# A prefetch hint for the closing jump of TensorE's loop over three experts

## The chip, the cores and the metric

The kernel runs on one core of one Trainium2 chip. The metric is the device time of one execution in microseconds (us). Engines are called as the profile calls them: TensorE (PE; PEld for its weight loads, PEldq for its sequencer's own instructions), VectorE (DVE), ScalarE (ACT), GpSimd (POOL) and SyncE (SP), which issues the large transfers.

## What is computed

A stream of 512 tokens by 1024 features goes through two layers. Layer 0 is a gated mixer over positions and then a mixture of experts; layer 1 is attention with forget gates and then a mixture of experts. The part around the change is the mixture of experts. Each token picks one of 4 groups and 2 of the 8 experts in it:

```python
def expert_block(args):
    xb, e = args
    hid = jax.nn.silu(xb @ w1[e]) * (xb @ w3[e])
    return hid @ w2[e]
```

There are 32 experts in each layer. An expert's w1 and w3 are 1024 by 512, its w2 is 512 by 1024, all in float32: 2 MB each, 6 MB for an expert.

## The kernel before

The dense parts (the mixer, the keys and values, the attention) are written out, with weights streamed through a ring of buffers. After each of them comes the expert stage, `moe_pe(l)` on TensorE (line 1418).

**Items.** VectorE sorts the tokens by expert and cuts each expert's tokens into items of at most 32 (`CAP`). It leaves the number of the first item of each expert in a small table, `n0_i`. Items run in order over all experts; this input gives 94 items in the two layers.

**TensorE's loops.** `expert(s, loads, r0, r1)` (line 1472) is a loop over the items r0 to r1 of one expert, with bounds read from the table. One pass does four things: the up-projection of item n by w1 and w3 (line 1479), the scatter of an earlier item's rows back to the tokens (`move_items`, line 1450), the gather of item n+1 (line 1468), and the down-projection of item n (line 1490). ScalarE and VectorE make the gated hidden values meanwhile. Expert 0 has its own copy of that loop; then comes the loop that the change touches (line 1520): 10 passes, each over 3 experts, so three copies of the item loop in its body, and, ahead of each, the load of its bounds from the table (lines 1497 and 1500). Line 1520 also names the closing jump. Expert 31 has a copy of its own after it, with 12 filler matmuls ahead (line 1313, `keep_busy`). The stage is built once for each layer, so the loop stands in the program twice and runs 20 passes.

**The weights.** Three buffers (`NBUF`) hold an expert's 6 MB each. SyncE loads expert e into buffer e mod 3 as soon as the expert three before it is through with it (line 403):

```python
sp.wait_ge(m["up"], ended)
sp.dma_start(w1_sb[s], w1e).then_inc(m["w13"][s], 16)
sp.dma_start(w3_sb[s], w3e).then_inc(m["w13"][s], 16)
sp.wait_ge(m["down"], ended)
sp.dma_start(w2_sb[s], w2e).then_inc(m["w2"][s], 16)
```

TensorE waits for `w13` before each item's up-projection and for `w2` before its down-projection. The first three experts' weights are loaded before the stage begins.

Of the kernel before, what the change touches and what calls it, by code (L numbers as in the profile page):

```python
# [38 lines left out]
NE = NG * EPG  # L39
# [10 lines left out]
NBUF = 3  # L50
# [7 lines left out]
def trunk(nc, x_in, a_norm, a_w_in, a_b_in, a_v_norm, a_w_s, a_b_s, a_w_out, kv_norm, kv_w, kv_b_f, k_norm,  # L58
          b_norm, b_w_qg, q_norm, b_w_out, m_norm, m_w_group, m_b_group, m_w_expert, m_b_expert,
          m_w1, m_w3, m_w2, out):  # L60
    with ExitStack() as ctx:
# [311 lines left out]
        def slot(e):  # L373

            return (e + 1) % NBUF
# [931 lines left out]
        def _(pe):  # L1307
# [110 lines left out]
            def moe_pe(l):  # L1418
# [53 lines left out]
                def expert(s, loads, r0, r1, gather_last=False):  # L1472
                    with pe.Fori(r0, r1) as n:

                        pe.wait_ge(m["w13"][s], 32 * loads)
                        pe.wait_ge(m["xT"], n + 1)
                        for k in range(KD):
                            for g in range(CG):
                                last = mm(ps[0][g * CAP:(g + 1) * CAP, 0:2 * P].rearrange("p (w n) -> p w n", w=2),  # L1479
                                          xT[:, k, :], w13_sb[s][:, :, k, g * P:(g + 1) * P], start=k == 0, stop=k == KD - 1)  # L1480
                        last.then_inc(m["up"], 1)
                        move_items(n)
                        if not gather_last:
                            gather(n + 1)
                        pe.wait_ge(m["hidT"], n + 1)
                        pe.wait_ge(m["w2"][s], 16 * loads)

                        for c in range(KE):
                            for g in range(CG):
                                last = mm(ps[2][g * CAP:(g + 1) * CAP, CW:2 * CW], hidT[:, c, :],  # L1490
                                          w2_sb[s][:, c, g * CW:(g + 1) * CW], start=c == 0, stop=c == KE - 1)
                        last.then_inc(m["down"], 1)
                        if gather_last:
                            gather(n + 1)

                def start_of(e):
                    return pe.value_load(n0_i[0:1, bass.ds(e, 1)], min_val=0, max_val=MAX_ITEMS - 1)

                def end_of(e):
                    return pe.value_load(n0_i[0:1, bass.ds(e + 1, 1)], min_val=1, max_val=MAX_ITEMS)  # L1500
# [16 lines left out]
                                  start=i == 0, stop=i == 2 * NT - 1)  # L1517
                last.then_inc(slot_w_done, 1)
                expert(slot(0), 1, 0, first_end)
                with pe.Fori(0, (NE - 2) // NBUF) as r:  # L1520
                    ended = start_of(r * NBUF + 1)
                    for s in range(NBUF):
                        first, ended = ended, end_of(r * NBUF + s + 1)
                        expert(slot(s + 1), r + (s + 1) // NBUF + 1, first, ended)
# [70 lines left out]
            for n in range(2):  # L1595
                for c in range(2):
# [3 lines left out]
                    for t in range(NT):  # L1600
# [10 lines left out]
                        last.then_inc(out_done, 1)  # L1611
            router_end(0)
            moe_pe(0)


# [163 lines left out]
            for g in range(2, 2 * NT):  # L1779
                attend_out(g // NT, g % NT, 0, PAIRS)  # L1780
            router_end(1)
            moe_pe(1)


# [20 lines left out]
```

## Time and profile before

| | |
|---|---|
| median of 3 runs | 1584.24 us (1584.18 to 1585.37) |
| span of the profiled execution, first to last instruction | 1584.0 us |
| TensorE matmuls | 1476.6 us busy, 93% of the span |
| TensorE weight loads | 1002.0 us, 63% |
| VectorE | 980.7 us, 62% |
| ScalarE | 474.0 us, 30% |
| expert stage of layer 0, its item loops | about 324 to 767 us |
| expert stage of layer 1, its item loops | about 1131 to 1571 us |
| bytes read and written in memory | 458.15 and 2.13 MB |

The profiled execution has no time of its own beside its span; the span stands 0.2 us below the median run. Busy shares of TensorE are of modelled ends: a busy TensorE need not be at its peak, and its sequencer's loads, jumps and register instructions are not counted in them. Instruction fetches are transfers too: the profile lists them as queues of the kind "instruction", and TensorE's are the packets of 16 KB on queue 8.

### The profile page before, as it was taken

The page shows a single profiled execution, that of the slowest core. Times are in us where ns is not written, and L with a number is a line of the kernel's source. Part 1 is how long each engine was busy: PE and PEld are TensorE (multiplying, and loading weights), DVE is VectorE, ACT ScalarE, POOL GpSimd, SP SyncE. Part 2 cuts the span into 40 slices and gives each one's busy share as a digit, 9 for nine tenths or more (in the row PEclk, how much of TensorE's full clock was granted, in tenths as well). Part 3 has the DMA queues.
Part 4 walks back from the last instruction along what each step waited for, and adds up shares of the span by engine and source line. Part 5 has one row for each costly group of instructions (what it writes and reads, how often), then busy time and mean ns, then how long its engine had stood idle before and what let it go on. Part 6 is the DMA issues. An engine that isn't in the chain of part 4 may idle for free.

```text
span 1584.0 us, 45784 instructions
## 1 busy us (share of the span) xinstructions
PE 1476.6 (93%) x18897; PEld 1002.0 (63%) x18898; DVE 980.7 (62%) x2114; ACT 474.0 (30%) x798; POOL 25.8 (2%) x64
## 2 busy tenths in 40 slices
PE   8999999999989989988999999989899897997978
PEld 6788888765555556545778875458655554554545
DVE  5346642377767767765744357852777675675755
ACT  6442221412222222221543355533222221221211
POOL 3000000000000000000000000000000000000000
PEclk9999999999999999998999999999999998999989
DMA  6331332989999999999431322125899999999996
GB/s 220 119 106 54 107 106 69 389 331 429 429 428 427 430 428 427 429 430 428 179 106 55 121 80 81 40 74 245 357 389 427 429 429 429 427 429 429 428 428 277
DMA packets 55482, 461.12 MB, mean 291 GB/s; under 512 B 4496, under 2 KB 4640, under 8 KB 30848
## 3 DMA queue, kind: packets, MB, share of 16 engines
q1 hardware_dynamic: 51728, 453.00, 69.0%
q10 hardware_dynamic: 2192, 4.23, 0.8%
q0 software_dynamic: 1504, 3.07, 0.7%
q8 instruction: 42, 0.69, 0.2%
q14 instruction: 16, 0.13, 0.0%
HBM read 458.15 MB, written 2.13 MB: 291 GB/s over the span
## 4 chain that ended last, share of the span: by engine, by line
PE 72%; DMA 22%; DVE 4%; issue 2%; SPq 0%; ACT 0%; DVEq 0%; ACTq 0%
DMA EB<-in_m_w 22%; PE ps L1479 15%; PE ps L1317 10%; PE ps L1319 10%; PE ps L1318 10%; PE ps L1468 7%; PE ps L1490 6%; PE ps L1450 4%; PE ps L1705 2%; PE ps L1740 1%; PE ps L1759 1%; PE ps L1774 1%; PE ps L1592 1%; PE ps L1313 1%; PE ps L1379 1%
## 5 line engine op out<-in xcount | busy, mean ns | idle before, releaser
L1479 PE MATMUL ps<-EB,SCR 128*32 128x256 f32 x6016 | 364.4, 397 | 72.5 <-DMA EB<-in_m_w 59.7
L1479 PEld LDWEIGHTS ps<-EB,SCR 128*32 128x32 f32 x6016 | 195.7, 114 | 233.4 <-issue 105.1
L995 DVE TENSOR_TENSOR X<-X,ps 128x1024 f32 x188 | 221.1, 1218 | 28.9 <-PE ps L1450 28.9
L1319 PE MATMUL ps<-EB_r 128*128 128x512 f32 x512 | 200.2, 391 | 0.0
L1468 PE MATMUL ps<-H,SCR 128*32 128x256 f32 x3072 | 185.6, 382 | 0.0
L1490 PE MATMUL ps<-EB,SCR 128*32 128x256 f32 x3008 | 179.5, 379 | 0.0
L666 ACT ACTIVATE SCR_r<-ps,SCR 128x256 f32 x94 | 44.5, 474 | 443.4 <-PE ps L1490 443.4
L986 DVE TENSOR_TENSOR SCR<-SCR,ps 128x128 f32<-128x128 f32 x94 | 37.0, 393 | 211.6 <-ACT SCR L663 211.6
L1490 PEld LDWEIGHTS ps<-EB,SCR 128*32 128x32 f32 x3008 | 97.7, 110 | 64.5 <-DVE SCR L989 0.4
L1318 PE MATMUL ps<-EB_r 128*128 128x512 f32 x352 | 137.5, 391 | 0.0
L1468 PEld LDWEIGHTS ps<-H,SCR 128*32 128x32 f32 x3072 | 90.4, 110 | 62.1
L1317 PE MATMUL ps<-EB_r,H_r 128*128 128x512 f32 x320 | 126.8, 396 | 1.4 <-DVE EB L1084 1.0
L1450 PEld LDWEIGHTS ps<-SCR_r 32*128 32x128 f32 x3136 | 99.8, 184 | 44.6 <-issue 44.6
L1318 PE MATMUL ps<-EB_r,H_r 128*128 128x512 f32 x320 | 124.7, 390 | 0.0
L1450 PE MATMUL ps<-SCR_r 32*128 32x256 f32 x3136 | 119.6, 290 | 3.7 <-DVE col L983 2.1
L663 ACT ACT_TABLE_LOAD x94 | 120.6, 1283 | 2.0 <-ACT SCR L659 0.3
L1319 PEld LDWEIGHTS ps<-EB_r 128*128 128x128 f32 x512 | 96.3, 188 | 20.5
L663 ACT ACTIVATE SCR<-ps 128x128 f32<-128x128 f32 x94 | 26.1, 278 | 245.3 <-PE ps L1479 245.3
L971 DVE SCALAR_TENSOR_TENSOR SCR_r<-SCR,item_slot,SCR_r 128x256 fp32r<-128x256 f32 x192 | 84.6, 482 | 14.8 <-DVE SCR_r L968 14.7
L857 DVE TENSOR_TENSOR EB_r<-EB,EB_r 128x1024 fp32r<-128x1024 f32 x56 | 65.1, 1220 | 38.2 <-ACT EB_r L625 38.2
L1317 PE MATMUL ps<-EB_r 128*128 128x512 f32 x192 | 77.4, 403 | 3.6 <-DVE EB_r L1288 3.5
L1318 PEld LDWEIGHTS ps<-EB_r 128*128 128x128 f32 x352 | 66.5, 189 | 12.6
(280 smaller groups left out, 1667.0 us busy)
## 6 DMA issues: line engine op xcount, KB each, us to landing
EB<-in_m_w SPq DMA_DIRECT2D x192, 2048.0 KB, 26.9
EB<-in_a_w_in SPq DMA_DIRECT2D x7, 2048.0 KB, 8.2
EB<-in_a_w_out SPq DMA_DIRECT2D x4, 2048.0 KB, 7.9
EB<-in_kv_w SPq DMA_DIRECT2D x4, 2048.0 KB, 12.6
EB<-in_b_w_qg SPq DMA_DIRECT2D x4, 2048.0 KB, 7.9
EB<-in_b_w_out SPq DMA_DIRECT2D x2, 2048.0 KB, 9.4
X<-in_x SPq DMA_DIRECT2D x4, 512.0 KB, 6.9
EB<-in_a_w_in SPq DMA_DIRECT2D x4, 512.0 KB, 9.7
```

What stands on the lines that cost most here:

```text
L663: a.activation(silu, ps[0][:, 0:P], ACT.Silu).then_inc(m["silu"], 1)
L666: a.activation(y_parts[:, bass.ds(n & 1, 1), 0, :], ps[2][:, CW:2 * CW].unsqueeze(1), ACT.Copy, scale=slot_w[:, bass.ds(n, 1)]).then_inc(m ...
L857: v.tensor_tensor(ring_lo[j][:, 2 * q:2 * q + 2, :], ring[j][:, 2 * q:2 * q + 2, :], ring_hi[j][:, 2 * q:2 * q + 2, :].bitcast(F32), ALU.s ...
L971: v.scalar_tensor_tensor(dst[:, i, :], toks[1], item_slot[:, bass.ds(items[i] + 2, 1)], dst[:, i, :].bitcast(F32), ALU.is_equal, ALU.add). ...
L995: add = v.tensor_tensor(X_t, X_t, moved[1][:, :, t, :], ALU.add)
L1317: mm(o, left[0], right[0], start=start, stop=False)
L1318: mm(o, left[0], right[1], start=False, stop=False)
L1319: return mm(o, left[1], right[0], start=False, stop=stop)
L1450: last = mm(moved[banks][:, g, t, :], sides[rows, i, t * P:(t + 1) * P], y_parts[rows, i, k, :], start=first and i == 0 and k == 0, stop=( ...
L1468: last = mm(ps[1][g * CAP:(g + 1) * CAP, 0:CW], S[:, c, :], H[:, c * D + g * CW:c * D + (g + 1) * CW], start=c == 0, stop=c == NT - 1)
L1479: last = mm(ps[0][g * CAP:(g + 1) * CAP, 0:2 * P].rearrange("p (w n) -> p w n", w=2), xT[:, k, :], w13_sb[s][:, :, k, g * P:(g + 1) * P], ...
L1490: last = mm(ps[2][g * CAP:(g + 1) * CAP, CW:2 * CW], hidT[:, c, :], w2_sb[s][:, c, g * CW:(g + 1) * CW], start=c == 0, stop=c == KE - 1)
```

## The change

TensorE's loop over three experts is now made by the general loop builder for that one engine, with a flag that marks the loop's closing jump as likely taken. The loop's bounds and its body are the same.

```diff
                 expert(slot(0), 1, 0, first_end)
-                with pe.Fori(0, (NE - 2) // NBUF) as r:
+                with nc.Fori(0, (NE - 2) // NBUF, engines=[pe.engine], hint_back_edge=True) as r:
                     ended = start_of(r * NBUF + 1)
```

In the built program this is one instruction more at the head of each of the two loops, and nothing else on any engine. The place is TensorE, from the end of expert 0's item loop (line 1473) into the head of the loop (line 1520, then the load of the first bound, line 1497):

```order
 L1473 COMPARE_AND_BRANCH
 L1520 UNCONDITIONAL_BRANCH
+L1520 BRANCH_PREFETCH_HINT
 L1520 ISA
 L1497 TENSOR_LOAD n_i
```

The hint stands inside the loop, so it runs on each pass. It names the compare-and-branch that closes the loop. That one, with the third expert's item loop ahead of it and the code that follows the exit, stands as before (TensorE, changed program; `ISA` rows are register instructions):

```order
L1479 MATMUL ps<-EB,SCR 32x256 x32
L1457 ISA
L1450 MATMUL ps<-SCR_r 128x256 x32
L1465 REGISTER_ALU
L1468 MATMUL ps<-H,SCR 32x256 x16
L1486 REGISTER_ALU
L1490 MATMUL ps<-EB,SCR 32x256 x16
L1473 REGISTER_ALU
L1473 COMPARE_AND_BRANCH
L1520 REGISTER_ALU
L1520 COMPARE_AND_BRANCH
L1525 TENSOR_LOAD n_i
```

Nothing moved here. The body holds three such item loops of 96 matmuls, 288 in all as the program writes them.

## Rows read from the trace of the kernel before

**Rows 1.** The page: the span, and the chain that ended last, by engine.
```profile
span 1584.0 us, 45784 instructions
...
PE 72%; DMA 22%; DVE 4%; issue 2%; SPq 0%; ACT 0%; DVEq 0%; ACTq 0%
```

**Rows 2.** Busy time by stretch; the last three numbers are PEclk, DMA share, GB/s.
```profile
343.00:348.00 5.00, 5.00 (x108) 3.17 (x104) 3.41 (x9) 1.37 (x2) 0.00 (x0) 1.00 0.39 108
348.00:374.00 26.00, 26.00 (x508) 15.67 (x504) 20.60 (x44) 6.10 (x9) 0.00 (x0) 1.00 1.00 426
...
707.00:753.00 46.00, 36.74 (x636) 20.91 (x632) 25.42 (x56) 8.13 (x12) 0.00 (x0) 0.89 1.01 430
...
1150.00:1155.00 5.00, 5.00 (x108) 3.17 (x104) 3.42 (x8) 0.72 (x2) 0.00 (x0) 1.00 0.42 121
```

**Rows 3.** Timeline of SyncE, 340 to 352 and 1140 to 1156 us: start, duration.
```profile
345.75 0.34 SPq L412 DMA_DIRECT2D EB<-in_m_w  x1
...
1152.11 0.33 SPq L412 DMA_DIRECT2D EB<-in_m_w  x1
```

**Rows 4.** TensorE's waits over the span: us in total, times, longest.
```profile
PE ps L1479 <- DMA EB<-in_m_w: 59.7, 18, 4.9
```

**Rows 5.** Transfers from 367 to 753 us: all queues, and the weight loads' issues.
```profile
DMA packets 11356, 165.42 MB, mean 429 GB/s; under 512 B 1260, under 2 KB 1260, under 8 KB 1260
...
q1 hardware_dynamic: 11356, 165.42, 100.7%
...
EB<-in_m_w SPq DMA_DIRECT2D x78, 2048.0 KB, 26.9
```

**Rows 6.** Timeline of TensorE at line 1479: start, duration, idle before in brackets.
```profile
333.59 0.64 PE L1479 MATMUL ps<-EB,SCR 128*32 128x256 f32 x8 [0.79 <-issue]
...
376.25 3.66 PE L1479 MATMUL ps<-EB,SCR 128*32 128x256 f32 x64 [1.05 <-issue]
...
712.14 2.36 PE L1479 MATMUL ps<-EB,SCR 128*32 128x256 f32 x20 [4.37 <-DMA EB<-in_m_w]
...
726.82 1.51 PE L1479 MATMUL ps<-EB,SCR 128*32 128x256 f32 x12 [4.89 <-DMA EB<-in_m_w]
...
1139.94 3.66 PE L1479 MATMUL ps<-EB,SCR 128*32 128x256 f32 x64 [0.73 <-issue]
```

**Rows 7.** The chain that ended last, in order of time, both layers' ends: start, us.
```profile
726.82 6.23 PE ps L1479 x64
...
737.80 3.55 PE ps L1479 x64
...
754.39 2.88 PE ps L1313 x24
...
1533.25 5.35 PE ps L1479 x64
```

**Rows 8.** Line 1520 on TensorE's sequencer: ns min/median/max, first and last start.
```profile
L1520 PEldq FUSED_REGOPS  x20: 73/73/73, 331.7 to 1513.4; - x20
...
L1520 PEldq COMPARE_BRANCH  x20: 73/216/221, 374.1 to 1558.8; - x20
L1520 PEldq MOVE  x2: 35/35/35, 331.6 to 1138.0; - x2
```

**Rows 9.** Line 1497, the loads of a first bound, the same view.
```profile
L1497 PEldq TENSOR_LOAD <-n_i x22: 297/304/319, 331.9 to 1560.7; - x22
...
L1497 PEldq SEQ_ASSERT  x22: 18/18/18, 332.5 to 1561.2; - x22
```

**Rows 10.** Transfers from 1174 to 1559 us: the one queue listed.
```profile
q1 hardware_dynamic: 11318, 164.94, 100.6%
```

**Rows 11.** Transfers from 754 to 780 us: the queue of TensorE's instructions.
```profile
q8 instruction: 3, 0.05, 0.8%
```

**Rows 12.** Busy time by stretch, as in rows 2: after the last waits for weights.
```profile
726.82:733.05 6.23, 6.23 (x68) 2.96 (x68) 0.00 (x0) 0.00 (x0) 0.00 (x0) 0.58 1.01 431
...
1533.25:1538.60 5.35, 5.35 (x68) 2.86 (x68) 0.00 (x0) 0.00 (x0) 0.00 (x0) 0.68 1.01 429
```

## The prediction

> **What bounds the kernel now.** I read four things in this order: the page's chain of waits, the transfer share by stretch, TensorE's own waits, and the sequencer's rows of the loop that is changed.
>
> The chain gives TensorE 72% of the span and the weight transfers 22% [rows 1]. That is a mean over different stages; the loop in question runs in the two expert stages, and what counts is which of the two ends last there. The stretches answer it. From 343 to 348 us the transfer engines are busy for 0.39 of the time, from 348 on for 1.00 and more, and still for 1.01 at the end of the loop, at 426 to 430 GB/s; layer 1 shows the same dip at 1150 [rows 2]. The dip ends when SyncE issues the next expert's weights at 345.75 and 1152.11 [rows 3], which it may do once TensorE has ended the last up-projection that used the buffer (line 408). So there is one moment in each layer, early in the first pass of the loop, at which the stream waits for TensorE. After it the stream is never empty, and TensorE waits for the stream: 18 waits, 59.7 us [rows 4].
>
> How far ahead is the queue? A load of 2048 KB (2.097 MB) takes 4.9 us at 429 GB/s by itself, but the median load of this stretch lands 26.9 us after its issue [rows 5], so some 22 us of other transfers usually stand in front of it. A TensorE that releases a buffer a microsecond late there delays nothing.
>
> The stage's last waits on the stream end at 712.14 after 4.37 us and at 726.82 after 4.89 us [rows 6]. From 726.82 in layer 0 and 1533.25 in layer 1 the chain runs on TensorE alone to the layer's end, across the loop's exit: filler matmuls of line 1313 at 754.39, then the last expert [rows 7].
>
> **What the change can save.** A prefetch hint saves something if the jump back waits for instructions. The loop's compare-and-branch runs 20 times: 18 jumps, median 216 ns, and two exits at 73 ns [rows 8]. So a taken jump costs 0.14 us more than one not taken. TensorE stands idle about 1 us at a jump (1.05 us at 376.25), but on entering the loop, where nothing jumps back, it also stands idle 0.79 us [rows 6]: most of that second is the head's two loads of loop bounds, 304 ns each on the sequencer [rows 9]. If the jump had to fetch instructions, the fetch would show in the instruction queue, and from 367 to 753 us that queue has no row at all; only the weight queue has one [rows 5]. Layer 1 is the same from 1174 to 1559 [rows 10]. These stretches hold all 18 jumps, and the fetches resume after the exit, three blocks between 754 and 780 [rows 11]. The whole loop stays in TensorE's instruction memory, and the jump finds its target there.
>
> Here a rule can be weighed against the rows. The Trainium skill (Runtime: NRT & Kernel Launch, "Instruction fetch mechanics") says that prefetch is purely sequential in blocks of 256 instructions, and that a taken branch whose target is outside the current window of two pages stalls for a fetch. The body has 288 matmuls as the program writes them, each with a weight load, so at least 576 instructions, more than two such blocks; by that rule each jump would fetch. The trace does not agree: no fetch stands in either stretch [rows 5, 10]. By the rows the sum below holds; by that rule a redirected prefetch would also miss at the exit, once in each layer, which is rival A's sum.
>
> So the saving of fetch time is nothing. If the hint made a taken jump as cheap as one not taken, it would give 18 x 0.14 = 2.6 us of TensorE's time, all of it before the waits at 712.14 and 726.82 and their like in layer 1, so those waits grow by as much and the end does not move. I cost it at nothing; its cover is the full weight stream.
>
> **What it adds.** One instruction at the head of each pass, 20 in all, on TensorE's sequencer. The trace of before has no such instruction. Bounds from rows of the same sequencer: 18 ns (SEQ_ASSERT) to 304 ns (a load of a loop bound) [rows 9]. I take 73 ns, the register instruction that stands right behind it in the loop's head [rows 8], as it is nearest in kind and place. Below nothing is excluded at the entry, where there is no jump to shorten.
>
> Of the 20, the 18 after a jump are covered as said: 18 x 0.073 = 1.3 us, shorter waits for weights. Two, one in each layer, run on entering the loop, before the dip of the stream ends; there TensorE waits for its own sequencer (0.79 us, "issue", and 0.73 in layer 1 [rows 6]), then runs two items to the release at 345.75. That is on the path: the stream, and with it everything after, starts later by the hint's time. Sum: 2 x 0.073 = 0.15 us, with bounds 2 x 0.018 = 0.04 and 2 x 0.304 = 0.6 us. The new instruction also moves the code behind it by one place; no fetch is waited for anywhere that I can see, so nothing.
>
> The profiled span is 1584.0 us [rows 1] and the median run 1584.24; 0.2 us lie around the span, or between executions. 1584.24 + 0.15 = **1584.4 us**. The three runs shown reach 1585.37, so the forecast's own range is 1583.5 to 1585.8. A difference under 0.2%, 3.2 us, is about what a measurement of this kernel can't tell from no change.
>
> **Rival A, slower: the exit misses.** The hint says that the jump is likely, and it is fixed, so it says so in the tenth pass too. If the prefetcher follows it and gives up the blocks behind the loop, the code after the exit has to be fetched when it is reached. The place is bad: from the exit to the layer's end TensorE is the chain [rows 7] and nothing covers a stall. Price: the three fetches after the exit took 0.8% of 16 engines over 26 us, 1.1 us each [rows 11]; the upper bound is a whole 2048 KB load alone, 4.9 us. One miss in each layer gives 2.2 to 9.8 us, 1586.6 to 1594.2; at 2 us each, 1588.4. It counts as slower from 1.6 us a miss. Against it: the exit of before needs no fetch, and with the loop resident the blocks behind it should be too. Chance 0.10, of it 0.07 beyond 0.2%.
>
> **Rival B, slower: the hint fetches anyway.** If it loads the loop's first block again on each pass, though it is there, 20 blocks join a stream that has no spare time. By bytes it is little: 0.05 MB for three blocks [rows 11], 0.33 MB for 20, 0.8 us at 429 GB/s, 1585.2. If all fall on one of the 16 engines, whose share every load needs, it is up to 20 x 1.1 = 22 us, 1606. Chance 0.05, of it 0.04 beyond 0.2%.
>
> **Rival C, faster: the clock after the last wait.** The first up-projection after the wait at 726.82 takes 6.23 us where 3.55 is usual, and in layer 1 5.35 us [rows 7]; the granted clock there is 0.58 and 0.68 as a mean, a mix of 1.2 and 2.4 GHz, after TensorE had stood idle [rows 12]. These 2.7 + 1.8 = 4.5 us lie on the chain. If the new instruction shifts work so that both vanish, the time is 1584.4 - 4.5 = 1579.9. Against it: the hint shortens those idle times by a tenth of a microsecond at most. Chance 0.03.
>
> That the change does nothing at all is within the forecast: the built program has the instruction, and if the chip ignores it the time is 1584.2.
>
> **How the numbers follow.** Forecast 0.82, A 0.10, B 0.05, C 0.03. Same: 0.82 + 0.03 of A + 0.01 of B = 0.86. Slower: 0.07 + 0.04 = 0.11. Faster: 0.03. The range runs from 1583.0, below the forecast's own range by half a microsecond, to 1587.8, which takes in the cheaper half of A.
>
> **What would show it.** Right: one more sequencer row on line 1520, 20 times; no instruction fetch between 367 and 753 us; the idle time before 333.59 longer by about 0.1 us, the weight stream resuming as much later, the waits for weights 1 to 2 us less in sum. The 216 ns may fall; the end should not follow. Wrong: instruction packets inside the loop (B), an idle time of over 1 us before the last expert or inside it (A), or full clock right after the last wait (C).

## The result, and the profile after

The changed kernel takes 1587.77 us (median of 16 runs, 1584.02 to 1591.79), the kernel before on the same chip 1585.01 us (median of 16, 1583.59 to 1585.93). The ratio is 1.0018 with a 95% interval of 1.0011 to 1.0025: slower by 2.8 us (1.7 to 4.0). That is under the 0.2% which the prediction set as its bound, but the interval leaves out no change. The forecast of 1584.4 us was too low.

The profiled execution took 1588.12 us, with 1.7 us around its span. In every later profile the same 1.7 to 1.9 us lie around the span, so the 1584.0 us of before [rows 1] would belong to an execution of some 1585.8 us, at the upper end of its runs, and the prediction's 0.2 us around the span were a comparison of two executions. The page of the changed kernel, its span and the chain by engine:

```profile
span 1586.4 us, 45804 instructions
...
PE 71%; DMA 22%; DVE 4%; issue 2%; SPq 0%; ACT 0%; DVEq 0%; ACTq 0%
```

There are 20 instructions more, and the shares are those of before within 1%. A page of shares can't show a loss of 0.2%. The sequencer's own rows of line 1520 show what was added (ns min/median/max, then first and last start):

```profile
L1520 PEldq BRANCH_PREFETCH_HINT  x20: 31/31/55, 331.5 to 1514.3; - x20
L1520 PEldq FUSED_REGOPS  x20: 73/73/73, 331.6 to 1514.4; - x20
...
L1520 PEldq COMPARE_BRANCH  x20: 87/233/247, 373.9 to 1559.5; - x20
```

The hint takes 31 ns. The closing jump has not become cheaper: median 233 ns against 216 [rows 8], and the one not taken 87 ns against 73.

On entering the loops, the timeline of TensorE at line 1479, and that of SyncE at the release which ends the dip of the stream:

```profile
333.44 1.93 PE L1479 MATMUL ps<-EB,SCR 128*32 128x256 f32 x32 [0.89 <-issue]
...
1141.04 2.34 PE L1479 MATMUL ps<-EB,SCR 128*32 128x256 f32 x37 [0.85 <-issue]
```
```profile
345.60 0.34 SPq L412 DMA_DIRECT2D EB<-in_m_w  x1
...
1153.20 0.33 SPq L412 DMA_DIRECT2D EB<-in_m_w  x1
```

TensorE stands idle 0.89 and 0.85 us, where it was 0.79 and 0.73 [rows 6]: 0.10 and 0.12 us more. From this matmul to the release it is 12.16 us in both layers, and before it was 12.16 and 12.17 (345.75 - 333.59 and 1152.11 - 1139.94 [rows 3, 6]), so the stream resumes later by just what the entry lost.

In the middle of the stage nothing is new. TensorE's waits over the span (us in total, times, longest), and all the queues that moved data from 367 to 752 us:

```profile
PE ps L1479 <- DMA EB<-in_m_w: 56.6, 17, 6.3
...
PE ps L1479 <- issue: 16.9, 15, 1.5
```
```profile
q1 hardware_dynamic: 11325, 164.98, 100.7%
```

The waits for weights are 3.1 us shorter than the 59.7 us of [rows 4]. That can't be put down to the hint: four kernels of the experiments below whose exits lose nothing have 52.3 to 54.8 us of such waits. The stream is as full as before [rows 5], and no instruction is fetched inside the loop. From SyncE's first instruction for the later loads (line 412, at 327.0 us in layer 0 of before) to the end of the last wait for weights a stage took 399.8 and 399.9 us in the two layers, and now takes 400.2 and 399.8.

The loss is behind the exit. First the kernel before, the timeline of TensorE at the first up-projection of expert 31 in layer 0 and in layer 1:

```profile
757.20 3.66 PE L1479 MATMUL ps<-EB,SCR 128*32 128x256 f32 x64
...
1562.74 3.66 PE L1479 MATMUL ps<-EB,SCR 128*32 128x256 f32 x64
```

The same of the changed kernel:

```profile
756.42 1.93 PE L1479 MATMUL ps<-EB,SCR 128*32 128x256 f32 x30
759.81 2.35 PE L1479 MATMUL ps<-EB,SCR 128*32 128x256 f32 x34 [1.46 <-issue]
...
1563.59 1.93 PE L1479 MATMUL ps<-EB,SCR 128*32 128x256 f32 x31
1566.62 2.13 PE L1479 MATMUL ps<-EB,SCR 128*32 128x256 f32 x33 [1.10 <-issue]
```

64 matmuls that ran as one group now break in two: after 30 (31 in layer 1) TensorE stands still for 1.46 and 1.10 us. "issue" means that nothing which the profile shows explains the wait. That the instructions themselves were not there is read from the instruction queue below. The chain of the changed kernel puts this idle time on the path that ends the layer (start, us, what):

```profile
756.49 1.86 PE ps L1479 x30
758.35 1.46 issue
759.81 2.35 PE ps L1479 x34
```

The instruction queue gives the reason. From 331 to 380 us, the entry and the first pass of layer 0, first before and then after:

```profile
q8 instruction: 5, 0.08, 0.6%
```
```profile
q8 instruction: 4, 0.07, 0.5%
```

From 752 to 760 us, around the exit, before has no row of this queue. After has one:

```profile
q8 instruction: 1, 0.02, 0.9%
```

It starts between 757 and 758 us:

```profile
q8 instruction: 1, 0.02, 6.9%
```

So one block of instructions that the first pass used to fetch along with the loop is not fetched now, and one is fetched behind the exit instead, just ahead of the idle time that begins at 758.35. In layer 1 the first pass (1137 to 1190 us) also has 4 such packets, where before had 5.

How much of the time is that? A measure that needs no reading of idle times is the stretch from the start of the closing compare that falls through to the first matmul of the next stage (line 1352) in layer 0, and to the last matmul of line 1530 in layer 1. Before it is 17.06 and 16.82 us, after 18.95 and 18.42: 1.9 and 1.6 us more. With the 0.2 us at the entries that makes 3.7 us, while the span grew by 2.4 us only: between two single executions other stretches differ by a microsecond or two as well. Means over several profiles come with the experiments.

### The profile page after: what moved, and what is told of

Read it like the earlier page. It is cut to its first block, busy times and chain, and to the rows that moved or that the text cites. A ratio compares the mean times of both kernels' runs of the same rounds, so it can differ in the third digit from the quotient of the medians.

```text
span 1586.4 us, 45804 instructions
## 1 busy us (share of the span) xinstructions
PE 1477.2 (93%) x18897; PEld 1001.9 (63%) x18898; DVE 980.9 (62%) x2114; ACT 474.4 (30%) x798; POOL 25.9 (2%) x64
## 4 chain that ended last, share of the span: by engine, by line
PE 71%; DMA 22%; DVE 4%; issue 2%; SPq 0%; ACT 0%; DVEq 0%; ACTq 0%
DMA EB<-in_m_w 22%; PE ps L1479 15%; PE ps L1317 10%; PE ps L1319 10%; PE ps L1318 10%; PE ps L1468 7%; PE ps L1490 6%; PE ps L1450 4%; PE ps L1705 2%; PE ps L1740 1%; PE ps L1759 1%; PE ps L1774 1%; PE ps L1592 1%; PE ps L1313 1%; PE ps L1379 1%
## 5 line engine op out<-in xcount | busy, mean ns | idle before, releaser
L971 DVE SCALAR_TENSOR_TENSOR SCR_r<-SCR,item_slot,SCR_r 128x256 fp32r<-128x256 f32 x192 | 84.6, 482 | 14.8 <-DVE SCR_r L968 14.7
```

The costliest lines, as they stand in the source:

```text
L971: v.scalar_tensor_tensor(dst[:, i, :], toks[1], item_slot[:, bass.ds(items[i] + 2, 1)], dst[:, i, :].bitcast(F32), ALU.is_equal, ALU.add). ...
```

## The experiments

**The place, and one instruction more.** If an added instruction or moved code were the cause, any cheap instruction in the hint's place would do the same.

```diff
-                    ended = start_of(r * NBUF + 1)
+                    pe.reg_mov(spare_reg(nc, pe), 0); ended = start_of(r * NBUF + 1)
```

> In place of the hint the head of the loop has a register move of one instruction, so the code behind it is shifted by one place exactly as by the hint. Exit theory (the pending hint keeps the block behind the loop from being fetched ahead): no idle time inside the up-projection of the last expert, and about 0.2 us over the kernel before (one more instruction at each of the two entries). Placement theory (one more instruction moves the code against the fetch blocks): the idle times of 1.46 and 1.10 us stay and the time is 2.5 to 3 us over the kernel before. Cost-per-pass theory (20 instructions of 0.1 us on the path): about 2 us over, without the idle times.

Measured: 1584.20 us against 1584.24, ratio 1.0001 (0.9992 to 1.0010). Expert 31's first up-projection in layer 0 is whole:

```profile
757.58 3.66 PE L1479 MATMUL ps<-EB,SCR 128*32 128x256 f32 x64
```

So it is neither one more instruction nor the shift of the code by one place. The entries lose nearly as much with the move as with the hint: TensorE stands idle 0.86 and 0.84 us there, 0.07 and 0.11 us more than in [rows 6].

**One layer alone.** The flag is set in one of the two built loops only.

```diff
-                with nc.Fori(0, (NE - 2) // NBUF, engines=[pe.engine], hint_back_edge=True) as r:
+                with nc.Fori(0, (NE - 2) // NBUF, engines=[pe.engine], hint_back_edge=l == 0) as r:
```

> The hint stands in layer 0 only. Exit theory: TensorE stands idle over 1 us inside the last expert's up-projection in layer 0 and not in layer 1; 1.3 to 1.7 us over the kernel before, about half of the whole change. Placement theory: layer 1's code is shifted by one place too, so both idle times stay and the time is that of the whole change.

Measured: 1587.48 us against 1584.24, ratio 1.0018 (1.0009 to 1.0027). The timeline at the exits of layer 0 and layer 1:

```profile
757.38 1.93 PE L1479 MATMUL ps<-EB,SCR 128*32 128x256 f32 x30
759.89 2.35 PE L1479 MATMUL ps<-EB,SCR 128*32 128x256 f32 x34 [0.58 <-issue]
...
1563.91 3.66 PE L1479 MATMUL ps<-EB,SCR 128*32 128x256 f32 x64
```

And with `l == 1`:

> The hint stands in layer 1 only. Exit theory: idle time of over 1 us inside the last expert's up-projection in layer 1 and none in layer 0; from the exit to the last matmul of line 1530 about 18.4 us where the kernel before has 16.8; 1 to 2 us over the kernel before. If layer 0's hint alone makes the whole difference, as its run alone suggests (3.2 us), layer 1's makes none and the time is that of the kernel before.

Measured: 1586.11 us against 1584.75, ratio 1.0006 (0.9997 to 1.0015), an interval that holds no change.

```profile
756.86 3.66 PE L1479 MATMUL ps<-EB,SCR 128*32 128x256 f32 x64
...
1562.20 1.93 PE L1479 MATMUL ps<-EB,SCR 128*32 128x256 f32 x31
1564.90 2.10 PE L1479 MATMUL ps<-EB,SCR 128*32 128x256 f32 x33 [0.78 <-issue]
```

The break stands in the layer that has the hint, and at the same matmul each time (30 and 31). The group is whole in the other layer, though its loop comes from the same builder, only without the flag; so the builder is not the cause. The idle time itself varies from one execution to the next, 0.6 to 1.5 us in these.

**The same again.** No edit to the changed kernel, and then none to the version with layer 0 alone, since the two layers' costs did not add up well.

> The changed kernel as it is, beside the two with one hint, on one chip. If the two exits add up, its excess over the kernel before is that of layer 0 alone plus that of layer 1 alone, 3 to 5 us, and a second profile shows idle time in the last expert's up-projection in both layers, of 0.5 to 1.5 us each. If the idle time is a matter of chance, one of the two layers can be without.

Measured: 1588.66 us against 1584.75, ratio 1.0024 (1.0014 to 1.0034). Both exits break as before, with 0.19 and 0.71 us of idle time.

> The hint in layer 0 only, once more, since its first run gave 3.2 us and its profile only about 1.1 us between exit and end of layer 0. If the exit is all that it costs, 0.8 to 2.2 us over the kernel before, with a stretch from exit to end that is longer by as much in the profile. If layer 0's hint costs elsewhere too, again about 3 us.

Measured: 1587.16 us against 1584.69, ratio 1.0017 (1.0008 to 1.0026). In this profile the group at the exit of layer 0 isn't broken in two, but it takes 4.32 us where 3.66 is usual, and the longest pause between the starts of two of its matmuls stands behind the 30th:

```profile
757.97 4.32 PE L1479 MATMUL ps<-EB,SCR 128*32 128x256 f32 x64
```

With these, the exit stretch of layer 0 is 18.95, 18.09, 17.69 and 17.55 us in the four profiles with the fixed hint at the head of its loop (mean 18.07), and 16.88 to 17.06 in six others (16.98: without a hint there, or with one of the two forms below). In layer 1 it is 18.42, 17.92 and 17.89 us in three with it (18.08), and 16.78 to 16.94 in the seven others (16.84). So a miss costs 1.1 us in layer 0 and 1.2 in layer 1; with 0.1 us for each entry that is 2.5 us, of the 2.8 and 3.9 us measured for both layers together. Layer 1 alone costs 1.24 + 0.12 = 1.36 us by the mean stretch and 1.36 us by the medians; that they agree so well is luck, with an interval as wide as that one. Layer 0 alone costs 1.2 us by the stretch and 2.5 to 3.2 us by the medians, whose intervals begin at 1.3 us; what the rest is, if it is more than chance, stays open.

How much one exit loses follows from how late its block comes. The times of the packets in the traces put its start 3.5 to 4.8 us behind the start of the closing compare in these seven exits. Against the means of the others, 0.6 and 0.7 us are lost where it is 3.5, 1.1 us where it is 4.0 to 4.3, and 1.6 and 2.0 us where it is 4.7 and 4.8. Why the fetch starts so late is not shown.

Part of the scatter between executions lies elsewhere than at the exits. In layer 1's attention TensorE waits 3.1 us for VectorE, up to about 1055 us, in before and with the register move alike. From 1050 to 1062 us its granted clock is then 0.86 as a mean, a mix of 1.2 and 2.4 GHz, in eight of the ten profiles of a loop over three experts, and 1.00 in two (the register move, and the hint on another loop below). First the changed kernel, then the register move:

```profile
1050.00:1062.00 12.00, 8.87 (x41) 6.36 (x38) 5.99 (x16) 2.56 (x7) 0.00 (x0) 0.86 0.00 0
1050.00:1062.00 12.00, 8.13 (x47) 6.12 (x45) 6.39 (x16) 2.88 (x7) 0.00 (x0) 1.00 0.00 0
```

From the first matmul of the next stage (line 1352) to the exit of layer 1 it is 788.1 to 788.5 us in the eight and 786.6 and 786.7 in the two. All four profiles with layer 0's fixed hint are among the eight, but so are four of the other six; whether the hint makes this more frequent is not shown.

**The hint late.** The hint stands directly ahead of the add and compare that close the loop. It still runs in every pass.

For this the loop is written out by a helper of its own:

```diff
-                with pe.Fori(0, (NE - 2) // NBUF) as r:
+                with hinted_loop(nc, pe, (NE - 2) // NBUF, "late") as r:
...
+        yield nc.snap(i, min_val=0, max_val=n - 1)
+        if when == "late":
+            at = pe.mark_branch_hint_location()
+        nc.regs_alu(i, i, 1, op=ALU.add)
+        pe.br_lt(i, n, on_true=name + "_loop", on_false=name + "_end").branch_hint(at)
```

> The hint stands directly ahead of the add and the closing compare-and-branch, not at the loop's head, and runs as often. Exit theory: by then the prefetch of the next block has been started, so the block behind the loop is there: no idle time in the last expert, fetches as before, time within 0.3 us of the kernel before. If the hint does its harm by what it does at the branch itself, whenever it came, the idle times stay and the time is 2.5 to 3 us over.

Measured: 1584.68 us against 1584.24, ratio 1.0003 (0.9994 to 1.0012). No break at the exit, and the first pass (331 to 380 us) again fetches five blocks:

```profile
756.48 3.66 PE L1479 MATMUL ps<-EB,SCR 128*32 128x256 f32 x64
```
```profile
q8 instruction: 5, 0.08, 0.6%
```

The fifth of them lies between 367 and 368 us, and the hint first runs at 374.5. A hint that comes when the block behind the loop has been fetched takes nothing away.

**The hint with an outcome from a register.** The hint stays at the loop's head, but it says "likely" in nine passes and "not likely" in the tenth.

It is made by the same helper:

```diff
-                with pe.Fori(0, (NE - 2) // NBUF) as r:
+                with hinted_loop(nc, pe, (NE - 2) // NBUF, "unless last") as r:
...
+        if when == "unless last":
+            last = nc.alloc_registers(name + "_last", engines=engines)
+            nc.regs_alu(last, i, n - 1, op=ALU.is_ge)
+            at = pe.mark_branch_hint_location(hint=list(last)[0])
...
+        pe.br_lt(i, n, on_true=name + "_loop", on_false=name + "_end").branch_hint(at)
```

> The hint stands at the head of the loop but takes its outcome from a register: likely taken in the first nine passes, likely not taken in the tenth. Exit theory: in the tenth pass the prefetch goes straight on, so no idle time in the last expert; two more instructions at the entries, 0.2 to 0.5 us over the kernel before. If the harm were in the first pass (blocks not fetched there), the idle times and about 2.5 us stay.

Measured: 1585.50 us against 1584.24, ratio 1.0007 (0.9998 to 1.0016). Its timeline at the entry and at the exit of layer 0, and the instruction queue from 753 to 754 us:

```profile
334.82 0.42 PE L1479 MATMUL ps<-EB,SCR 128*32 128x256 f32 x4 [1.00 <-issue]
...
757.27 3.66 PE L1479 MATMUL ps<-EB,SCR 128*32 128x256 f32 x64
```
```profile
q8 instruction: 1, 0.02, 6.9%
```

This tells most of all. Four blocks are fetched in the first pass, as in the changed kernel, and the fifth at the exit. But it comes between 753 and 754 us, within a microsecond of the closing compare (753.18), where in the changed kernel it came at 757 to 758, with the compare at 752.50. Expert 31's first up-projection is whole, and the exit stretch is 17.05 and 16.82 us, that of before. The block comes in time when the hint tells the truth in the last pass. So it is the wrong "likely" in the tenth pass that costs, not the hint's presence. No run here has a hint from a register that says "likely" in every pass; that the two forms do alike is seen in the first pass here and, below, at the jumps of the loop of six experts. The idle time at the entry is 0.2 us above [rows 6] in each layer, for two instructions more; the remaining 0.8 us of the median lie within the interval.

**The hint on another loop.** Only the item loop of expert 31 (line 1473) has the flag, the loop over three experts is plain.

```diff
-            with pe.Fori(r0, r1) as n:
+            with nc.Fori(r0, r1, engines=[pe.engine], hint_back_edge=gather_last) as n:
```

> The loop over three experts has no hint; the item loop of expert 31, which runs on by falling through its closing jump, has one at its head. Exit theory: the same miss at another place: no idle time inside the last expert's up-projection, but over 0.5 us of idle time or a stall of the sequencer in the code behind that loop (lines 1490 to 1540 and what follows), in each layer, 1 to 4 us over the kernel before in all. If the miss belongs to the loop over three experts alone, the time is that of the kernel before.

Measured: 1585.21 us against 1584.75, ratio 1.0001 (0.9991 to 1.0010). The expectation missed: no break and no lost time. Where the loop ends TensorE waits anyway, for VectorE:

```profile
768.21 1.22 PE L1450 MATMUL ps<-SCR_r 32*128 32x256 f32 x32 [1.43 <-DVE SCR_r L1000]
```

The fetches of layer 0 are those of before, too. In layer 1 they are not: from 1560 to 1572 us before has two packets, and this run has one. Its second starts after 1572 us, 14.7 us behind the exit from the loop over three experts, where in the six profiles of the loop of three without a fixed hint at its head in layer 1 (the hint on another loop aside) it is 11.2 to 11.8. So in layer 1 a block came some 3 us late and nothing waited for it (the exit stretch is 16.94 us); in layer 0 no miss shows.

**A loop whose jump does fetch.** Where would the hint be worth its price? The body is made to hold six experts, 5 passes instead of 10, without the hint and with it.

```diff
-                with pe.Fori(0, (NE - 2) // NBUF) as r:
-                    ended = start_of(r * NBUF + 1)
-                    for s in range(NBUF):
+                with pe.Fori(0, (NE - 2) // (2 * NBUF)) as r:
+                    ended = start_of(r * (2 * NBUF) + 1)
+                    for s in range(2 * NBUF):
...
```

> The loop takes six experts in a pass, five passes, no hint: a body of twice the instructions. If TensorE's instruction memory still holds it, TensorE's idle time at a jump stays at 1.0 to 1.1 us and no instruction packet of queue 8 stands between the first pass and the exit. If the body is now too long for it, each pass fetches its blocks again (some 8 packets of queue 8 in each of five passes), and the jump shows idle time of 2 us or more. The time moves by under 3 us either way, since the jumps lie before the waits for weights.

Measured: 1603.25 us against 1584.29, ratio 1.0114 (1.0097 to 1.0131). The closing jump of the plain loop of six, TensorE's timeline behind its first jump, and the instruction queue from 380 to 752 us:

```profile
L1520 PEldq COMPARE_BRANCH  x10: 73/6114/6262, 407.7 to 1576.7; - x10
```
```profile
415.76 2.79 PE L1479 MATMUL ps<-EB,SCR 128*32 128x256 f32 x24 [6.97 <-issue]
```
```profile
q8 instruction: 43, 0.70, 0.8%
```

The eight taken jumps take 6.0 to 6.3 us, some twenty-eight times the 216 ns of [rows 8], and 43 blocks are fetched inside the loop in layer 0. In the trace an item is 160 matmuls (64, 32, 32 and 32) with as many weight loads, so the body of three experts holds 960 of these, that of six 1920. The first stays in the instruction memory and the second does not. The Trainium skill (Runtime: NRT & Kernel Launch, "Instruction fetch mechanics") says that a taken branch to a target outside the window stalls for a fetch; the body of six agrees with it, at 6.1 us a jump, while the 960 instructions of the body of three do not fit its two pages of 256 and run without a fetch. The same section gives TensorE's instruction memory 2048 instructions. By that figure the body of three fits, as the trace has it; the body of six, with 1920 matmuls and weight loads and its register instructions beside them, lies close to the figure, and it did not stay.

The expectation that the time would move under 3 us missed. From SyncE's first instruction of line 412 to the end of the last wait for weights the stages took 409.4 and 408.0 us, where it is 399.8 and 399.9 in before. In layer 0 the stream ran short once, behind the third jump (610 to 620 us, DMA share 0.75), which is worth some 3 us. In layer 1 it was full throughout, and the stage grew by 8 us all the same:

```profile
610.00:620.00 10.00, 10.00 (x198) 5.99 (x194) 8.22 (x17) 2.03 (x3) 0.00 (x0) 1.00 0.75 287
1164.00:1550.00 386.00, 340.87 (x6265) 199.99 (x6256) 258.00 (x557) 81.13 (x119) 0.00 (x0) 0.94 1.01 426
```

So the stalls at the jumps explain only a small part of it, as far as these rows show. What every stage of a loop of six has is some 40 blocks of instructions more, which share the transfer engines with a stream that has no spare time. That is the cost which the prediction named in rival B. Over this run and the two below, the growth without those 3 us is 0.16 to 0.20 us for each added block, between rival B's 0.04 by bytes (0.8 / 20) and its 1.1. No run tests this by itself.

> The same with the hint. If the body of six experts does not fit, this is the loop that the hint is for: the idle time at a jump falls back to about 1.2 us, while the exit still misses, with over 0.5 us of idle time in the last expert's up-projection of each layer, and the time is not below that of the loop of six without a hint. If the body fits, it differs from that one as the changed kernel from the kernel before, by 2 to 4 us.

Measured: 1608.95 us against 1584.29, ratio 1.0156 (1.0139 to 1.0173). The ten closing compares, then the first two and the last two jumps of layer 0, the idle time behind one of these, and expert 31's first up-projection in layer 0:

```profile
L1520 PEldq COMPARE_BRANCH  x10: 90/396/5099, 408.8 to 1576.7; - x10
...
L1520 PEldq COMPARE_BRANCH  x2: 2747/2796/2846, 408.8 to 498.0; - x2
...
L1520 PEldq COMPARE_BRANCH  x2: 366/375/384, 594.2 to 674.7; - x2
```
```profile
596.62 2.78 PE L1479 MATMUL ps<-EB,SCR 128*32 128x256 f32 x45 [1.35 <-issue]
600.72 1.49 PE L1479 MATMUL ps<-EB,SCR 128*32 128x256 f32 x19 [1.31 <-issue]
...
769.51 2.50 PE L1479 MATMUL ps<-EB,SCR 128*32 128x256 f32 x23 [3.01 <-issue]
```

Here the hint does a part of its work. The 396 ns are a median over ten compares, two of which fall through. Of the eight jumps four, the last two of each layer, take 0.37 to 0.41 us, and the other four 2.7 to 5.1. The idle time behind the four short ones falls from 7 to 1.3 or 1.4 us, with a second gap of 0.4 to 1.3 us in the same up-projection; at the others it is 3.7 to 5.8. The stage to its last wait for weights falls from 409.4 to 406.3 us in layer 0 and by 1.9 us in layer 1. And yet the kernel is slower than without the hint, because both exits miss: the exit stretch is 21.98 and 20.10 us, against 16.88 and 16.81 in the plain loop of six. That is 8.4 us lost at the exits for 3.1 and 1.9 us gained in the stages. The remaining 3.4 us are what the two profiled spans differ by (1605.2 and 1601.9 us); the medians differ by 5.7, and the profiled run is the shortest of its four.

The last run is this loop with the outcome from a register, as in the experiment above ("not likely" in the fifth pass).

> The loop of six experts, its hint taken from a register: likely taken in four passes, likely not taken in the fifth. The jumps keep what the hint gives them (idle time of 1.3 to 5.8 us in place of 7). Exit theory: the stretches from the exit to the layer's end, 22.0 and 20.1 us with the fixed hint, fall back to about 17, so the time is 7 to 9 us below the loop of six with the fixed hint and a few us below the one without a hint, about 1600 to 1602 us. If the exits cost for another reason, it stays at 1607 to 1610.

Measured: 1601.91 us against 1584.69, ratio 1.0104 (1.0088 to 1.0119), a time as expected. The jumps are those of the fixed hint (four at 0.37 to 0.39 us, four at 2.9 to 4.8), and the exit is whole, with a wait for weights ahead of it:

```profile
L1826 PEldq COMPARE_BRANCH  x10: 73/390/4774, 408.3 to 1574.0; - x10
```
```profile
764.43 3.66 PE L1479 MATMUL ps<-EB,SCR 128*32 128x256 f32 x64 [0.93 <-DMA EB<-in_m_w]
```

The exit stretches are 17.89 and 18.25 us, not the 17 of the expectation; 0.93 and 1.32 us of them are such waits for weights, which the plain loop of six does not have there. The excess over before is 17.2 us, and with the fixed hint it was 24.7: some 7 us for one bit of the hint in the last pass. Against the loop of six without a hint (1.0114, 1.0097 to 1.0131) the two intervals overlap, so a gain over it is not shown. No version with a hint beat the kernel before.

## Why the prediction was wrong

**What bounds the kernel**: held. The stream sets the time up to the last wait for weights, TensorE alone from there to the layer's end. That is why 18 hints and 18 dearer jumps in the middle cost nothing that the stages show (400.2 and 399.8 us against 399.8 and 399.9), and one stall behind the exit costs all of itself.

**What the change can save**: held. No fetch inside the loop before or after, and the jump is not shorter. The rule that the prediction weighed against the rows is half of what its source says: in that section of the Trainium skill (Runtime: NRT & Kernel Launch, "Instruction fetch mechanics") the window of two pages stands beside 2048 instructions for TensorE's memory. The trace agrees with the second figure: the body of three, 960 matmuls and weight loads, stays.

**What it adds**: at the entries the mechanism held and the size was low. Each entry lost 0.10 and 0.12 us where 0.073 was taken; the bounds of 0.018 and 0.304 hold it. The hint's own 31 ns are less than that, and the 29 ns of the register move in its place lost 0.07 and 0.11; the rest of the entry's loss was not traced. The shorter waits for weights that were named as a sign can't be told from scatter.

**Rival A is what happened**, at a chance of 0.10. The step that failed is the sentence against it: "the exit of before needs no fetch, and with the loop resident the blocks behind it should be too." With it a fetch at the exit went into the sum at nothing ("no fetch is waited for anywhere that I can see"), where it measured 1.1 and 1.2 us, 2.3 of the 2.5 us that the traces show. In before they were there, but because something fetched them: in the first pass one block more comes in than with the hint (five against four), and that one is the block which the exit needs. In these runs a block behind the loop is there because it was fetched ahead, and the fixed hint at the loop's head takes that fetch away. I had looked at the stretches with the jumps, where the queue has no row [rows 5, 10], and at the blocks that come after the exit [rows 11], but not at the fetches of the first pass, where the block of the exit arrives. That the missing fifth block is the one behind the loop is read from three things that fit (four against five, one at the exit, the pause at the same matmul each time); the trace gives no addresses.

Its price was right at the lower end: 1.1 to 4.9 us a miss was the forecast, 1.1 and 1.2 us the mean, 0.6 to 2.0 in single exits. It is under the "2 us each" that I put in the middle: the block starts 3.5 to 4.8 us behind the closing compare and takes 1.1 us, and the first 2.8 to 3.2 us of that delay are not seen in the exit stretch; in that time TensorE still runs the filler matmuls and the first 30 or 31 matmuls of the up-projection.

**Rival B** did not happen: no instruction packet from 367 to 752 us. **Rival C** did not show: the exits of the versions without a miss take the 16.8 to 17.1 us of before. The range of 1583.0 to 1587.8 just holds the 1587.77; that is no merit of the sum behind 1584.4, only of the cheaper half of rival A, which it took in.

## What to carry to other kernels

Look first whether the jump waits for instructions at all: its own duration (216 ns or 6.1 us here) and the instruction queue inside the loop say so, and where they showed nothing, in the loop of three, no form of the hint gained anything. Then look at the exit, and at whether the path to the end runs across it: a hint that says "likely" in the last pass too leaves the code behind the loop unfetched, and 1.1 to 1.2 us in each layer, or 3 to 5 us in the larger loop, fall on whoever ends last. Where the jump does stall, a hint that takes its outcome from the loop's counter is right in every pass: in the loop of six it was some 7 us better than the fixed one, though not shown to be better than none. The body of three, which is not fetched again, was better than all of them.

## What was not expected of the hardware

A fixed hint at the head of a loop changes what is fetched in its first pass, not only at its jump: four blocks instead of five. Just ahead of the jump the hint changes nothing, with five blocks and 1584.68 us.

With the hint a jump back in the loop of six still takes 0.37 to 0.41 us in the last two jumps of each layer, and 2.7 to 5.1 in the first two, in place of 6.0 to 6.3.

Fetching instructions beside a full stream of weights goes with a longer stage, whether TensorE's stalls at the jumps are long or short. With 37 to 41 blocks more in a stage it grew by 6.2 to 9.5 us in the three versions of the loop of six. The rows of layer 0 show a full stream in the one with the fixed hint, first before and then that run:

```profile
348.00:726.00 378.00, 348.14 (x6604) 207.67 (x6596) 271.71 (x586) 85.16 (x125) 0.00 (x0) 0.99 1.01 428
348.00:733.00 385.00, 353.17 (x6608) 210.54 (x6596) 272.09 (x586) 85.15 (x125) 0.00 (x0) 0.98 1.01 426
```
